# First layer's rotations: partner rows moved by DMA instead of permutation products

## The reference, cut to what is computed

```
h = rmsnorm(x, g_pre); proj = h @ w_in      # qa ka va gate_a qi ki wi qb kb vb fb gate_b
qa, ka, qi, ki = partial_rope(...)          # first 16 of the 64 features of each head
score = sum_h wi[h] * relu(qi[h] . ki)      # index scores, causal
sel = top_k(score, 128)                     # keys kept for each query
att_a = attention(qa, ka, va) over sel;  att_b = forgetting attention(qb, kb, vb, fb)
y_a = (att_a * silu(gate_a)) @ w_branch_a;  y_b = (att_b * silu(gate_b)) @ w_branch_b
```

## Time and profile before

| | |
|---|---|
| median of 3 runs | 1424.48 us (1423.29 to 1425.48) |
| the profiled execution | 1426.11 us, of which the span is 1424.3 us |
| TensorE busy | 1303.5 us, 92% |
| VectorE busy | 665.3 us, 47% |
| ScalarE busy | 624.7 us, 44% |
| GpSimd busy | 454.6 us, 32% |

### The profile page before, as it was taken

One profiled execution on the slowest core, in us unless ns is written; L12 is line 12 of the kernel. 1 busy time (PEld: TensorE's weight loads), 2 busy tenths in 40 slices (PEclk: granted clock), 3 DMA queues, 4 the chain that ended last, 5 costly groups with the idle time before them and its releaser, 6 DMA issues.

```text
span 1424.3 us, 19580 instructions
## 1 busy us (share of the span) xinstructions
PE 1303.5 (92%) x7182; PEld 1011.8 (71%) x7182; DVE 665.3 (47%) x1270; ACT 624.7 (44%) x1327; POOL 454.6 (32%) x360
## 2 busy tenths in 40 slices
PE   7999799999999989969989999999989999999995
PEld 5677566677668667668767777787867778677774
DVE  3335981765512315263266567552623601565423
ACT  7334133655352235362136566654434422655432
POOL 3433143221244423270133333332342133222431
PEclk9999899999999999989999999999999999999998
DMA  5221243100242453442042522101143232121441
GB/s 212 89 87 61 89 148 121 58 30 31 89 148 90 173 196 119 148 148 74 24 115 54 153 51 69 43 31 60 59 165 123 96 124 84 62 87 60 178 118 60
DMA packets 27869, 139.87 MB, mean 98 GB/s; under 512 B 4096, under 2 KB 5760, under 8 KB 15232
## 3 DMA queue, kind: packets, MB, share of 16 engines
q1 hardware_dynamic: 20640, 115.43, 23.9%
q10 hardware_dynamic: 7136, 23.19, 4.8%
HBM read 122.87 MB, written 6.29 MB: 91 GB/s over the span
## 4 chain that ended last, share of the span: by engine, by line
PE 69%; DVE 12%; ACT 8%; issue 4%; DMA 3%; POOL 3%; SPq 1%; ACTq 0%; DVEq 0%; POOLq 0%
PE psum L642 47%; PE psum L670 4%; POOL w_low L1168 2%; PE psum L781 2%; DMA w_raw<-stream 2%; ACT w_high L1318 2%; PE psum L874 2%; ACT q_masked L1339 2%; DVE arena L1968 1%; PE psum L999 1%; PE psum L630 1%; PE psum L860 1%; PE psum L1112 1%; PE psum L1126 1%; PE psum L712 1%
## 5 line engine op out<-in xcount | busy, mean ns | idle before, releaser
L1168 POOL TENSOR_TENSOR w_low<-w_raw,w_high 128x512 fp32r<-128x512 f32 x268 | 357.0, 1343 | 785.0 <-ACT w_high L1318 784.8
L1318 ACT CAST w_high<-w_raw 128x512 fp32r<-128x512 f32 x268 | 161.1, 621 | 369.9 <-PE psum L642 246.1
L642 PE MATMUL psum<-x_high,w_high 128*128 128x512 f32 x528 | 227.4, 431 | 20.5 <-DVE k_low L1973 8.9
L642 PE MATMUL psum<-x_low,w_high 128*128 128x512 f32 x528 | 212.1, 402 | 0.0
L642 PE MATMUL psum<-x_high,w_low 128*128 128x512 f32 x528 | 211.7, 401 | 0.0
L642 PEld LDWEIGHTS psum<-x_high,w_high 128*128 128x128 f32 x528 | 101.3, 192 | 67.6 <-issue 30.7
L642 PE MATMUL psum<-w_high,x_high 128*128 128x512 f32 x288 | 119.7, 416 | 5.7 <-DVE gate_b L2096 4.6
L642 PEld LDWEIGHTS psum<-x_high,w_low 128*128 128x128 f32 x528 | 101.2, 192 | 24.5
L642 PE MATMUL psum<-w_low,x_high 128*128 128x512 f32 x288 | 115.8, 402 | 0.0
L642 PE MATMUL psum<-w_high,x_low 128*128 128x512 f32 x288 | 115.4, 401 | 0.0
L642 PEld LDWEIGHTS psum<-x_low,w_high 128*128 128x128 f32 x528 | 101.3, 192 | 18.9 <-issue 1.4
(11 more groups left out here) (425 smaller groups left out, 2662.3 us busy)
## 6 DMA issues: line engine op xcount, KB each, us to landing
w_raw<-stream SPq DMA_DIRECT2D x98, 1024.0 KB, 4.9
x_kept<-arena ACTq DMA_DIRECT2D x8, 512.0 KB, 4.2
arena<-x_kept ACTq DMA_DIRECT2D x8, 512.0 KB, 5.5
arena<-bias ACTq DMA_DIRECT2D x8, 512.0 KB, 3.9
q_masked<-e_q_high SPq DMA_DIRECT2D x24, 96.0 KB, 2.3
arena<-x SPq DMA_DIRECT2D x4, 512.0 KB, 5.2
arena<-x ACTq DMA_DIRECT2D x4, 512.0 KB, 5.6
arena<-ctx ACTq DMA_DIRECT2D x4, 512.0 KB, 5.6
```

The costliest lines, as they stand in the source:

```text
L642: mm = pe.matmul(o, l, r, start=(first and n == 0 and kind != "fc"), stop=(last and n == len(passes) - 1))
L1168: pool.tensor_tensor(PLACE[u][1], RAW[:, g % 2, u % 4, :], PLACE[u][0].bitcast(F32), ALU.subtract).then_inc(w_lo, 1)
L1318: act.copy(PLACE[u][0], RAW[:, g % 2, u % 4, :]).then_inc(w_hi, 1)
```

## The change

The nine permutation products of the first layer go. SyncE moves the partner rows by DMA from SBUF to SBUF instead: four DMAs for a chunk, each of 8 partitions (and of all four tiles, for qi and qa), into `A_SWAPPED` or `K_SWAPPED`. These are cleared once at VectorE's start, since rows that don't turn are never written. VectorE turns a tile by two products in place and a sum. The rotations of qa are laid between the index sums, one instruction after each sum from `n = 4` on. Banks of the index stage begin at 2 instead of 0, and ga, gb and vb have rounds of their own: ga 2, 3, 0, 1 and guest 4; gb 5, 6, 7, 4 and guests 2, 3; vb 0, 1, 2, 5 and guests 6, 7. ScalarE copies the guest's row before the sigmoids. gate_a's product moves from after `n == 6` to after `n == 8`.

```diff
+        A_SWAPPED, K_SWAPPED = arena(5376, 4, S), A_R[:, 0, :]
-        ROPE_A = ([(A_KF[:, 0, :], ("keys", 0))]
-                  + [(q[:, j, :], (c, j)) for c, q in (("qi", A_QI), ("qa", A_QA)) for j in range(4)])
+        ROPE_A = ([("keys", A_KF[:, 0, :], K_SWAPPED)]
+                  + [(c, q[:, j, :], A_SWAPPED[:, j, :]) for c, q in (("qi", A_QI), ("qa", A_QA)) for j in range(4)])
...
             pe.wait_ge(sig("consts_in"), 16 * N_CONSTS)
-            pool[0] = APART
-            rotate("rope_a", ROPE_A[0:1], "perm_a")
+            pool[0] = (2,)
             consumed(pe, ("keys", 1))
             acc = next_bank(("vw", 0))
...
-            rotate("rope_a", ROPE_A[1:5], "perm_a", 1)
             pool[0] = ALL
             for k in range(2, NK):
                 unit("qa", k, X)
-            turn[ALL] += 5
...
-                score_pair([("i", i), ("i", i + 1)], (i % 4, i % 4 + 1), prep_of("i", pr), t,
+                b = (i + 2) % 4
+                score_pair([("i", i), ("i", i + 1)], (b, b + 1), prep_of("i", pr), t,
                            BH[:, 1, 0:w], BL[:, 1, 0:w])
...
-            pool[0] = LOWER
-            rotate("rope_a", ROPE_A[5:9], "perm_a", 5)
-            pool[0] = ALL
             pe.wait_ge(sig("mx"), 2)
+            pool[0] = (2, 3, 0, 1, 4)
             gemm("ga", X)
+            pool[0] = (5, 6, 7, 4, 2, 3)
             gemm("gb", X)
+            pool[0] = (0, 1, 2, 5, 6, 7)
             gemm("vb", X)
...
-            pool[0] = ALL
+            pool[0], turn[ALL] = ALL, 7
             gemm("mb0", X)
...
+            def swap(chunk, src, out):
+
+                for at in (0, 64):
+                    for a, b in ((0, 8), (8, 0)):
+                        sp.dma_start(out[at + a:at + a + 8], src[at + b:at + b + 8]).then_inc(sig(f"{chunk}_swapped"), 16)
...
+                if g == granule_of(UNITS["qi"][0]) + 2:
+                    sp.wait_ge(sig("swap_clear"), 1)
+                    consumed(sp, ("keys", 0))
+                    swap("keys", A_KF[:, 0, :], K_SWAPPED)
+                if g == granule_of(UNITS["qa"][0]) + 2:
+                    sp.wait_ge(sig("ct_hi"), 2)
+                    sp.wait_ge(sig("ct_lo"), 2)
+                    for j in range(4):
+                        consumed(sp, ("qi", j))
+                    swap("qi", A_QI, A_SWAPPED)
+                if g == granule_of(UNITS["qb"][0]) + 2:
+                    sp.wait_ge(sig("rope_a_out"), 5)
+                    for j in range(4):
+                        consumed(sp, ("qa", j))
+                    swap("qa", A_QA, A_SWAPPED)
                 if g >= 2 and GRANULES[g - 2][0] == "w":
...
             for c, g in (("ga", GA), ("gb", GB)):
                 ahead(c)
+                guest_rows(c)
                 for j in range(4):
                     ps = filled(act, (c, j))
                     act.activation(g[:, j, :], ps[:, :], ACT.Sigmoid).then_inc(sig(f"{c}_sig"), 1)
-                guest_rows(c)
...
             dve.memset(scr(95), 1.0).then_inc(sig("one"), 1)
+            dve.memset(A_SWAPPED, 0.0)
+            dve.memset(K_SWAPPED, 0.0).then_inc(sig("swap_clear"), 1)
+            dve.wait_ge(sig("swap_clear"), 1)
...
             def rope_a(i):
-                q, src = ROPE_A[i]
-                consumed(dve, src)
-                if i:
-                    dve.wait_ge(sig("rope_a_out"), i)
-                rope("rope_a", i, q, A_R)
+
+                chunk, q, swapped = ROPE_A[i]
+                dve.wait_ge(sig(f"{chunk}_swapped"), 64)
+                dve.tensor_tensor(q, q, TAB[:, 0, :], ALU.mult).then_inc(sig("rope_a_part"), 1)
+                yield
+                dve.tensor_tensor(swapped, swapped, TAB[:, 1, :], ALU.mult).then_inc(sig("rope_a_part"), 1)
+                yield
+                dve.wait_ge(sig("rope_a_part"), 2 * i + 2)
+                dve.tensor_tensor(q, q, swapped, ALU.add).then_inc(sig("rope_a_out"), 1)
+                yield
 
             for i in range(5):
-                rope_a(i)
+                for _ in rope_a(i):
+                    pass
...
-            summed = {}
+            summed, query_ropes = {}, (part for i in range(5, 9) for part in rope_a(i))
...
                 summed[t] = n
+                if n >= 4:
+                    next(query_ropes, None)
...
             dve.wait_ge(sig("idx_sum"), 3 * HEADS)
-            for i in range(5, 9):
-                rope_a(i)
...
-                if n == 6:
+                if n == 8:
                     gated("ga", GA)
```

More of the change, by code:

```diff
@@ L584, in open_two @@
                 return PS[:, 512 * b:512 * b + 1024]
-            ALL, LOWER, UPPER, LAST, APART = tuple(range(8)), tuple(range(4)), tuple(range(4, 8)), (6, 7), (2, 3, 4, 5)
+            ALL, LOWER, UPPER, LAST = tuple(range(8)), tuple(range(4)), tuple(range(4, 8)), (6, 7)
             APART_E = (0, 1, 2, 3, 6, 7)
```

## The result

The changed kernel takes 1406.28 us in the median (four executions, 1401.18 to 1409.97) against 1423.88 us before (four, 1422.79 to 1425.48): the ratio is 0.9873, 95% interval 0.9838 to 0.9908. The forecast was 1404, range 1400 to 1411. The profiled execution took 1404.51 us with a span of 1402.7, which is 21.6 us under the span before, for a forecast of 20.6.

What follows compares the result with a forecast made beforehand. TensorE, busy 92% of the span, was taken as the bound. Parts 1 to 3 gave 19.0 us; with Part 4 TensorE restarts 20.6 us earlier in all, so 1424.5 - 20.6 = 1403.9, forecast 1404, range 1400 to 1411.

Steps and rivals of the forecast that it cites:

- Parts 1 to 3: First five permutation products, last four with the hole behind kb, and slow clock after it: 4.30, 12.31 and 2.42, together 19.0 us.
- part 1: First five permutation products, between units of qa: all 4.30 us come off TensorE, and everything behind shifts together.
- Part 4: gate_b wait in vb: VectorE's chain ends after TensorE's, about 3.1 us of wait stays, TensorE restarts 20.6 us earlier in all.
- Moving gate_a from n == 6 to n == 8 is what keeps the 5.72 out: VectorE's maxima rounds: the later place of gate_a's product avoids VectorE's 5.72 us idle waiting for gate_a.
- the hole: TensorE's gap between qa's last four permutation products and ga's start at 155.84, with ga's first bank awaiting k_low.
- Part 2: Between kb and ga: dropping the last four products and giving ga banks 2, 3, 0, 1 saves all 12.31 us.
- (d): Index stage: twelve query-tile operations between sums bring VectorE to about 26 of 30.5 us, nothing on TensorE.
- Rival A: Index stage: VectorE fills up as rotations run into w_low, TensorE waits, rounds start late; 1406 to 1412, chance 0.12.
- (b): Twelve swap DMAs on SyncE's queue: 4.7 us from wait to data per set, landing estimated somewhat longer; cost taken as nothing.
- The clock: Behind gate_b's remaining 3.1 us wait: slow level as before, so it cancels; if not, 1.7 us more saved.

Runs made afterwards that it cites:

- e5: The kernel before with only the keys' and qi's rotations by DMA; qa's products, banks and gate_a as before: 1419.96 us, ratio 0.9967.
- e2: The changed kernel with gate_b's product on VectorE ahead of the three mask instructions instead of behind them: 1403.77 us.
- e3: The changed kernel with qa's rotations behind all index sums, still by DMA: 1413.02 us, ratio 0.9924.
- e4: The changed kernel with gate_a's product after n == 6 as before, instead of n == 8: 1406.38 us, ratio 0.9872.
- e6: The changed kernel with ga, gb and vb in one round of all eight banks as before: 1402.66 us, ratio 0.9847.
- e7: The changed kernel with the qi and qa swaps as sixteen DMAs each instead of four, same bytes: 1407.31 us, ratio 0.9887.
- e9: The changed kernel with ScalarE's casts of qi's units 3 to 6 between the forget-gate steps, gate_b behind the masks: 1401.36 us, ratio 0.9832.
- e1: The changed kernel measured again without any edit: 1403.69 us, ratio 0.9859.
- e8: The changed kernel with gate_b ahead of the masks and casts of qi's units 3 to 6 between the forget-gate steps: 1391.5 us, ratio 0.9768.
- e10: The e8 kernel with ScalarE's copy of the first index query ahead of qa's four copies: 1395.35 us, ratio 0.9784.

## Why the prediction was right, and where not

**Parts 1 to 3** (19.0 us) held. The first products were worth 4.3 us of TensorE and 4.6 us of time (e5). ga follows kb directly, at full clock. But not "all" shifts together, as part 1 had it: VectorE's rotations of qi stand behind the transposes, which did not move by the 4.3. The query came 4.7 us earlier and VectorE ended 1.4 us later, so 0.83 us are left of its 6.88 ahead of the first query.

**Part 4** held to 0.1 us: gate_b forecast at 194.2 and found at 194.21, TensorE's restart at 195.0 and 194.96, wait 3.1 and 3.14. So close an agreement is partly luck: k_low came 0.3 us early, and the way from it to gate_b took 0.3 us more. The mechanism is shown by e2 and e3. It was a race of two chains, and VectorE's ended later than TensorE's at this place: 2.3 us off VectorE's chain took 2.3 off the wait, 8.8 on it put in waits of 7.4 for 3.1.

**"Moving gate_a from n == 6 to n == 8 is what keeps the 5.72 out" was wrong.** With n == 6 the idle was 1.01 us (e4). The 5.72 were there because ga had started late behind the hole; with ga directly behind kb its sigmoids come about as early as round 7 ends. It cost the forecast nothing, since n == 8 was the case.

**Part 2's account of the banks was right as a mechanism and wrong in weight.** ga's names do take away its wait, but the hole closes by VectorE's earlier k_low alone, down to 2.45 us, and the wait at gate_b goes for it (e6).

**(d), the index stage:** taken at 26 us of VectorE in 30.5, measured 23.21 for the sums and twelve rotation operations; no new wait of TensorE. Rival A fell. The twelve added 7.9 us, 0.66 each: that is the prediction's low end (0.7), although its argument from GpSimd's w_low sent (d) to the high end (1.28). The lock that the Trainium skill names (SBUF — State Buffer, "Who interferes with whom") is to be seen, though. In the index stage two of the four sine products took 1.77 us for a usual 0.68, with w_low beside them:

```profile
104.07 1.77 DVE L2058 TENSOR_TENSOR arena<-arena,tables_sb 128x512 f32<-128x512 f32 x1
```

The rotation operation at 77.11 took 1.67 us, and the masks took 1.14 us in e4 beside 2.30. In the index stage the pauses of VectorE hid it, and it did not decide.

**(b), the swaps:** hidden, as taken. I had not seen that VectorE's own rotations of qi leave only 0.83 us ahead of the first query; e7 tested that. How long the eight-row DMAs take to land was not timed: the last of qi's was issued at 58.4, and VectorE started on its rows at 62.36 without waiting.

**The clock** was the term that was mis-sized. I took it as 1.7 us either way at one wait. It also falls in mid attention where no wait is over 1 us, in the profiles of e2, e7 and e9 and not in the others. The changed kernel's executions spread over 8.8 us, with the mean clock lowest in the slowest. The median of the first four is 17.6 us under the kernel before, while the profile's span is 21.6 under it and e1's median 20.5. So the forecast of 1404 for a measured 1406.28 has a share of luck: single executions reach 1409.97, near the end of the range. The slower executions of the changed kernel may have the dip in mid attention; it is not shown, since neither of its two profiles has it. What decides whether the clock falls there is not settled: e2 and e9 start attention at other times than the changed kernel, but so do e4 and e6, which have no dip.

Not tried: rotations between the sums with permutation products instead of DMAs. All eight banks are taken in the index stage, so it would need another layout; that the DMAs are necessary for the interleaving is argued, not shown. Nor were qa's four products, or ScalarE's earlier copy of the guest's row, tried by themselves; what they gave is known only within the 21.1 us.

## What to carry to other kernels

Follow the engine that is busy half the time through the stretch where it is busy all the time: here VectorE's order, not TensorE's products or the bank names, set TensorE's restart, and the 2.3 us that came off that chain (e2) came off the wait one for one. Place work of that engine in its earlier pauses, and put what frees a bank ahead of what nobody waits for yet. Judge an edit of a few microseconds at a mark in the trace close behind it; the time of the whole execution can hide it under a clock dip elsewhere.

## What the runs showed of the hardware that I had not expected

The granted clock was 0.76 over 14 us of attention with TensorE busy 82% and no wait over 1 us in it (e2), and 1.00 in the same stretch of another kernel with the same program there (e8). Behind waits of 2.35 us (e10) and 2.45 us (e6) it fell, behind one of 3.5 us (e4) it didn't. Behind the wait of 1.97 us at the first index query it fell in the changed kernel (0.68 over the next 4 us) and didn't in e8. So the length of a wait alone does not tell. A DMA of 64 KB that touches eight partitions was no trouble in the changed kernel: four of them were issued in 2.7 us, and VectorE never waited for them.
